# A group's one-hot matrices built in one run, and the coefficient matrix stored token by token

## The reference

```python
q = (xb @ w_pq).reshape(PEER_BLOCK, PEER_HEADS, 2, PEER_HALF)
s = jnp.einsum('nhpc,phkc->nhpk', q, pk_keys)
v1, i1 = lax.top_k(s[:, :, 0], PEER_TOPK)          # 16 of 128 keys, on each of two sides
v2, i2 = lax.top_k(s[:, :, 1], PEER_TOPK)
...                                                 # best 16 of the 256 sums, per head
eidx = jnp.take_along_axis(cidx, sel, axis=-1)      # i1 * 128 + i2, out of 16384 experts
g = jax.nn.softmax(sc, axis=-1)
a = jax.nn.gelu(jnp.einsum('nhkd,nd->nhk', peer_u[eidx], xb))
out = jnp.einsum('nhk,nhkd->nd', g * a, peer_v[eidx])
```

## Time and profile before

| | us |
|---|---|
| three runs | 4554.2, 4540.98, 4552.7 |
| the profiled execution | 4541.82 |
| its span | 4540.2 |
| TensorE (PE) products busy | 3830.6 (84%) |
| PE weight loads (PEld) busy, beside the products | 2304.7 (51%) |
| VectorE (DVE) busy | 2595.6 (57%) |
| GpSimd (POOL) busy, almost all of it issuing gathers | 1499.0 (33%) |
| ScalarE (ACT) busy | 724.2 (16%) |
| the stream's products, line 1731 | 1807.5 |
| the dots, line 1527 | 1304.3 |
| the filling's products, line 1713 | 339.7 |

### The profile page before, as it was taken

How to read it: one execution, slowest core, us unless ns; L and a number is a source line. 1 busy time by engine, 2 the same in 40 slices (tenths; PEclk the granted TensorE clock), 3 DMA queues, 4 the chain that set the end, 5 groups by cost and what they waited for, 6 DMA issues and landing times.

```text
span 4540.2 us, 40362 instructions
## 1 busy us (share of the span) xinstructions
PE 3830.6 (84%) x14392; PEld 2304.7 (51%) x14392; DVE 2595.6 (57%) x5470; ACT 724.2 (16%) x897; POOL 1499.0 (33%) x1247
## 2 busy tenths in 40 slices
PE   7999997999987990027999869999679998699998
PEld 6878874555557990025444354444454343544443
DVE  3111104434323888989978699797898786920000
ACT  3111112333421110024000050000330001500000
POOL 0000000000000477753656524656336564331100
PEclk9999997999998995568999989999899999899999
DMA  4222116233314799875999948999669998486654
GB/s 167 84 82 102 65 54 209 101 111 118 126 60 135 241 320 320 268 254 187 391 405 397 382 145 337 404 403 403 229 240 393 402 399 328 137 301 204 204 162 139
DMA packets 321866, 1068.09 MB, mean 235 GB/s; under 512 B 51665, under 2 KB 54801, under 8 KB 319601
## 3 DMA queue, kind: packets, MB, share of 16 engines
q0 software_dynamic: 179520, 654.00, 40.0%
q1 hardware_dynamic: 137712, 391.66, 23.9%
q10 hardware_dynamic: 4480, 20.45, 1.2%
HBM read 1003.20 MB, written 62.78 MB: 235 GB/s over the span
## 4 chain that ended last, share of the span: by engine, by line
PE 38%; DVE 13%; DMA 12%; POOL 3%; issue 2%; ACT 1%; SPq 0%; ACTq 0%; DVEq 0%
PE pair L1731 31%; DMA e_vr<-in_peer_v 10%; DVE e_ur L1527 5%; POOL e_ur L1275 3%; DVE e_sc L1607 3%; PE pair L1713 3%; PE pair L1685 2%; PE pair L1664 2%; DVE e_sc L1612 2%; DMA e_ur<-in_peer_u,e_eidx 2%; DVE e_oh L1596 0%; DVE e_sc L1434 0%; DVE e_oh L1601 0%; DVE e_oh L1598 0%; DMA e_sc<-sc_d 0%
## 5 line engine op out<-in xcount | busy, mean ns | idle before, releaser
L1731 PE MATMUL pair<-e_vr,e_region 128*128 128x512 f32 x4096 | 1807.5, 597 | 45.2 <-DMA e_vr<-in_peer_v 43.7
L1275 POOL DMA_INDIRECT e_ur<-in_peer_u,e_eidx x1088 | 1383.2, 1271 | 1252.9 <-DVE e_dots L1527 930.5
L1527 DVE CUSTOM_DVE_ANT_0 e_ur<-e_ur,e_h 128x1024 f32<-128x1024 f32 x1088 | 1304.3, 1222 | 297.2 <-DMA e_ur<-in_peer_u,e_eidx 288.3
L1731 PEld LDWEIGHTS pair<-e_vr,e_region 128*128 128x128 f32 x4096 | 762.1, 190 | 1079.7 <-issue 839.5
L1713 PE MATMUL pair<-e_sc 128*128 128x128 f32 x2048 | 339.7, 325 | 178.8 <-DVE e_sc L1607 149.4
L1713 PEld LDWEIGHTS pair<-e_sc 128*128 128x128 f32 x2048 | 304.9, 231 | 214.5 <-DVE e_sc L1607 181.5
L400 PE MATMUL pair<-w_hi,h_hi 128*128 128x512 f32 (+1 forms) x936 | 365.8, 391 | 0.7 <-issue 0.6
L400 PE MATMUL pair<-w_lo,h_hi 128*128 128x512 f32 (+1 forms) x936 | 365.1, 390 | 0.0
L400 PE MATMUL pair<-w_hi,h_lo 128*128 128x512 f32 (+1 forms) x936 | 364.6, 390 | 0.0
L1383 ACT ACTIVATE e_region<-pair 128x512 f32<-128x512 f32 x256 | 272.4, 1070 | 247.9 <-PE pair L1713 239.2
L148 DVE TENSOR_SCALAR e_n<-e_n 128x1 f32<-128x1 f32 (+1 forms) x9 | 1.4, 153 | 533.4 <-ACT e_n L143 533.4
(11 more groups left out here) (215 smaller groups left out, 2979.7 us busy)
## 6 DMA issues: line engine op xcount, KB each, us to landing
e_vr<-in_peer_v SPq DMA_DIRECT2D x512, 512.0 KB, 6.7
w<-in_w_in POOLq DMA_DIRECT2D x13, 2048.0 KB, 9.4
proj<-out_sb SPq DMA_DIRECT2D x104, 256.0 KB, 2.0
e_ur<-in_peer_u,e_eidx POOLq DMA_INDIRECT x1088, 8.3
V<-proj POOLq DMA_DIRECT2D x36, 256.0 KB, 3.0
gates<-proj SPq DMA_DIRECT2D x8, 1024.0 KB, 4.9
e_region<-in_w_pq SPq DMA_DIRECT2D x4, 2048.0 KB, 15.1
sc_d<-e_region ACTq DMA_DIRECT2D x16, 512.0 KB, 5.9
```

What stands on the lines that cost most here:

```text
L1275: pool.indirect_dma_start(ur[:, m % U_RING, :], None, peer_u[0], bass.IndirectOffsetOnAxis(ap=eidx[:, n % 3, k:k + 1], axis=0))\
L1527: dve.tensor_tensor_reduce(ur[:, m % U_RING, :], ur[:, m % U_RING, :], h2[:, n % 2, :], 1.0, 0.0, ALU.mult, ALU.add, dots[:, n % 2, k:k + ...
L1731: last = pe.matmul(acc[t][:, c], dense[:, t, i, :], vr[:, no % V_RING, c], start=False, stop=True, skip_group_check=True)
```

## The change

DVE no longer does dots inside the filling: all 64 batches of one-hots follow the codes of the group, behind dot k=1, and the dots k=2 to k=33 come after them. In the tiles of the fillings routing starts at k=6 with every fourth dot, as in the others. `dense` is stored with the token as the outer and the first key as the inner index: ACT's copy of a batch writes 512 contiguous elements where it wrote with a step of 128 elements (512 bytes), and PE's weight load for a slice reads its 128 columns with that step where it read them contiguously.

```diff
-        dense = region[:, :].rearrange("p (t i n) -> p t i n", t=2, n=P)
+        dense = region[:, :].rearrange("p (t n i) -> p t n i", t=2, n=P)
...
                         act.wait_ge(s["cb_mm"], g * BATCHES + m + 1)
-                        act.activation(dense[:, t, :, at:at + BATCH].rearrange("p i n -> p n i"),
+                        act.activation(dense[:, t, at:at + BATCH, :],
                                        cb_ps[m % 3].rearrange("p (n i) -> p n i", n=BATCH), ACT.Copy)\
...
                                 codes(g, 1)
                                 if g > 0:
                                     finish(2 * g - 1)
-                            elif 2 <= k < 2 + BATCHES // 2:
-                                hots(g, 2 * (k - 2))
-                                hots(g, 2 * (k - 2) + 1)
-                            elif n < LAST and k >= 36 and k % 3 == 0 and (k - 36) // 3 < PARTS:
-                                routing(n + 1, (k - 36) // 3)
-                        elif k >= 6 and k % 4 == 2 and (k - 6) // 4 < PARTS:
+                                for m in range(BATCHES):
+                                    hots(g, m)
+                        if n < LAST and k >= 6 and k % 4 == 2 and (k - 6) // 4 < PARTS:
                             routing(n + 1, (k - 6) // 4)
...
-                                last = pe.matmul(acc[t][:, c], dense[:, t, i, :], vr[:, no % V_RING, c], start=False,
+                                last = pe.matmul(acc[t][:, c], dense[:, t, :, i], vr[:, no % V_RING, c], start=False,
                                                  stop=True, skip_group_check=True)
```

## The result

The changed kernel took 4565.94 us (median of six runs, 4561.4 to 4567.91); the kernel before, run beside it, 4542.35 (4538.71 to 4554.2). The medians differ by 23.6 us. The ratio, formed from all runs of both, is 1.0043 with a 95% interval of [1.003, 1.0056] (brackets behind a ratio mean this throughout): 0.43% slower, some 20 us. The forecast was 4544 and no change. The change is clear of the interval, so "no change" fails, though the time lies in the stated range, which is 105 us wide. The profiled executions differ by 4563.2 - 4540.2 = 23.0 us of span, and these are what I take apart.

The account below looks back on a forecast made before the run. No single engine was taken to set the end: DVE bounds fillings, DMA the streams. Head -1, three periods +8 and last group -10 gave -3: 4539 on the profiled scale, 4550 on the median's, said 4544; range 4495 to 4600.

Parts of the forecast that it names:

- no change: Whole kernel: a time within 0.3%, about 14 us, which a measurement cannot tell from no change; chance 0.40.
- Filling: One-hot stage without its 32 dots: first product of the stream 96 us after the first mark, 129.5 before; ends 95 and 114.
- the start at the lower level: In the filling, PE starting at 1.2 GHz behind a pause: 1 us added, 95 to 96.
- the pause of 1.38: In today's filling, a pause in us followed by a load of 0.97 us, no clock drop; new pauses put at about 1.5.
- the cold filling: Rival: each 1.5 us pause drops PE's clock, filling up to 114, period +18, total +72, 4610; chance 0.19 for +15 to +72.
- Stretch: From filling's end to last dot: 32 added gathers at 403 GB/s, 505 us, 37 behind the stream; ends 497 and 512.
- Break: From last dot to the next first one-hot, for copies, norms and codes: 15.2 us.
- Weight load: Stream loads at a 512-byte step: 0.31 us against 190 ns today, hidden under the 429 ns cadence, cost 0.
- the doubling to 380 ns: Stream weight load: estimate from the skill's line rule that the whole load doubles, still under 429 ns.
- Routing: Even tiles, routing from k=6 every fourth dot, not k=36 every third: same parts and instructions, cost 0.
- Last group: Final group: filling saves 33 us, PE stalls 21 at its first weighing, clock restart costs 2; together -10.
- Sum: Whole kernel: head -1, three periods +8, last group -10, total -3; 4539 or 4550 by scale, said 4544.

Follow-up runs that it names:

- the halved bytes: The kernel before and the changed kernel, each loading only 512 of 1024 columns of every peer_v tile: 4481.12 us (0.985) and 4426.63 us (0.9739).
- Layout alone: The kernel before with only `dense` stored token by token, its order of dots kept: 4553.99 us, 1.0014 of the kernel before.
- weighing later: The changed kernel with the last group's weighing begun at slice 36, not 24: 4545.5 us, 0.9993 of the kernel before.
- the last group alone: The kernel before with one-hots built in one run only in the last group, and weighing from slice 36: 4516.88 us, 0.9939.
- spread one-hots: The changed kernel with small one-hots double-buffered, 16 tokens at a time, made between the batches: 4540.28 us, 0.9983 of the kernel before.

## Why the prediction was wrong

Its mechanism (a filling shortened, the gain given back to a stretch bound by transfers, a stall in the last group) is what the runs show. Its sum came out with the wrong sign because several small terms were too low, that of the filling most of all. By its steps:

*Filling: the step that failed.* "I count 1 us for the start at the lower level: 96." From the mark to the last copy it takes 102.0, 101.1, 100.2 and 100.6 us. The weight loads of the first filling, PE's timeline after, show why:

```profile
2010.65 0.97 PEld L1710 LDWEIGHTS pair<-e_sc 128*128 128x128 f32 x8 [1.88 <-DVE e_sc L1607]
...
2022.39 4.42 PEld L1710 LDWEIGHTS pair<-e_sc 128*128 128x128 f32 x24 [1.88 <-DVE e_sc L1607]
```

Both stand behind a pause of 1.88 us for the small one-hots. Behind the first a batch's eight loads took 0.97; behind the second 24 took 4.42, 1.47 a batch. The stage view of these two stretches has the granted clock (the seventh figure, after POOL):

```profile
2022.39:2026.81 4.42, 4.39 (x24) 4.42 (x24) 3.37 (x6) 1.19 (x2) 0.00 (x0) 0.61 0.00 0
2010.65:2015.00 4.35, 3.94 (x29) 3.49 (x30) 4.22 (x7) 1.79 (x3) 0.00 (x0) 1.00 0.00 0
```

0.61 against 1.00: PE came back at 1.2 GHz and rose to 2.4 on the way. VectorE's timeline shows a block (eight batches, between two instructions of this line) of the second filling at either speed, and the stage view of the two blocks their clocks:

```profile
2656.07 0.69 DVE L1596 TENSOR_TENSOR e_oh<-e_kT,cst 128x512 f32<-128x512 f32 x1
...
2667.88 0.69 DVE L1596 TENSOR_TENSOR e_oh<-e_kT,cst 128x512 f32<-128x512 f32 x1
...
2680.53 0.69 DVE L1596 TENSOR_TENSOR e_oh<-e_kT,cst 128x512 f32<-128x512 f32 x1
```

```profile
2656.07:2667.88 11.81, 9.04 (x65) 7.78 (x65) 11.45 (x20) 4.82 (x9) 0.00 (x0) 1.00 0.00 0
2667.88:2680.53 12.65, 10.22 (x64) 9.22 (x64) 11.59 (x20) 4.74 (x9) 0.00 (x0) 0.87 0.01 1
```

11.81 us and 12.65, where I had 11.6. In the four fillings the second to seventh blocks are 24: ten have a granted clock of 1.00 and take 11.74 to 11.81 us, fourteen have 0.87 and take 12.65 to 12.97. With every block at 11.74 (and the last, with its product and copy, at 13.57) a filling would take 95.7, close to my 95. The start at the lower level adds 1.4 in the first block, where I had 1; what I left out is 3.9 more on average in the first three fillings, some 1.1 for each later block in which the clock was down again. I took the pause of 1.38 without a drop for the safe one and reckoned new pauses of 1.5; the case that I priced as a rival, the cold filling, came at under a third of its bound. With the pauses gone (and the waits that went with them), the period is 615.9 and the kernel 27 us faster. 5.1 us too low, three times, and about as much once more in the last group.

*Stretch.* 505.0, 505.1 and 507.3 us, predicted 505. The rate is 398 and not 403, and the gathers alone at its end are faster than the 1.6 us each that I took (22 issued in the 30 us up to 2600, at 366 GB/s, 19 in the 29 us up to 3222, at 346): two errors that cancel, so that 505 came out right is in part luck. The stream ends 34 us ahead of the last dot, predicted 37. That this is where the filling's gain goes, the halved bytes show: take the bytes away, and the change gains 54 us.

*Break.* 16.2, 18.3 and 16.2 us, predicted 15.2. ACT's second copy waits 7.7 to 9.9 us for the store of the first tile's outputs. In the kernel before the same wait was 4.89, on ACT's timeline:

```profile
2606.39 1.02 ACT L1357 ACTIVATE e_x<-pair 128x1024 f32<-128x1024 f32 x1 [4.89 <-DMA out<-e_x]
```

The break is 1.7 us over the prediction on average. That gathers now share the DMA with this store is my reading; no run took them away, and the cause is not shown.

*Weight load.* 296 ns, predicted 310, hidden, and the cadence is unchanged. The Trainium skill (SBUF — State Buffer, "Door 1: The DMA port swizzle") has the direction right; the doubling to 380 ns, my estimate from it, isn't what the row shows: 106 ns more for 128 columns. Layout alone costs at most 0.27% by its interval, its middle 0.14% (6 us), and I had 0; a cost of a few us is neither shown nor excluded.

*Routing.* I put the move at 0. Left in its old place routing costs 17 us more, so the step hid a gain: the high rate that I took for the whole stretch rests on it.

*Last group.* Predicted -33 + 21 + 2 = -10, measured -2.2. The first product of the stream follows its mark after 100.6 us, 129.1 before: -28.4. From there to the first weighing 117.5 us, 93.4 before: +24.1, where I had 21. The restart and the rest: +2.1. The stall itself is shown by weighing later: 23 us.

*Sum.* Filling 3 x 5.1 = 15, break 5, stretch 2, last group 8, head -5 (scatter): 25 to 26 us more than -3, which is +23. The forecast's 4544 lay between two scales; against before's median beside it (4542.35) a sum of -3 is 4539, and the miss is 27 us. What I should have drawn from my own rows: three terms each with their uncertainty on the slow side (pauses, a shared store, a stall at the weighing) around a sum of nearly 0 are no forecast of "no change".

## What to carry over

Before moving work out of a stage because its engine is full, look at which resource of the next stage the moved work needs: here 32 dots fewer made a filling 28 us shorter, and their 16.8 MB came back on a DMA that was already full. Do it only where the next stage has that resource free or nothing there waits for the moved work (the last group alone gave 28 us). If it must move, moving half (16 dots) did better than moving all; that it does better than moving nothing isn't shown. Look at what consumes the result first, since a due time can be shifted for nothing (twelve slices, 23 us). When a stage gets shorter, read the granted clock behind each pause left in it (0.87 over a block went with some 1.1 us more here), and see whether the work that makes the pauses can go between other instructions.

## What the hardware showed that was not expected

- The same pause of 1.88 us was followed once by a granted clock of 1.00 and once by 0.61. Ahead of both PE had done the same batches of eight loads with gaps of 0.23 to 0.39 us. What decides between the two is not shown. In the filling with spread one-hots the mean granted clock was 0.96, in the one with pauses 0.90.
- An fp32 weight load of 128 columns takes 190 ns contiguous and 296 ns at a step of 512 bytes, (296 - 190) / 128 = 0.83 ns a column; an ACT write of 512 columns 597 against 1073 ns, 0.93 ns an element. The load's extra time cost nothing visible under records of 429 ns.
- Gathers through six buffers with no other transfer beside them moved 10.97 MB in the 30 us up to 2600, 366 GB/s, and 346 GB/s in the 29 us up to 3222, against 319 in the 40 us ahead of the first filling from which I had taken their rate.
